# Hybrid recurrent decoder step: first mixer's tiles, second mixer's preparation, first loads and a triangular inverse reordered

## The reference

```python
z = rms(x) @ w_in                      # columns of four mixers and 4 x 1024 merge gates
o_hg = gated linear recurrence (HGRN2) # S = diag(a) S + k v^T, by chunks
o_rw = RWKV-7 delta rule               # S = S diag(w) - (S kk)(kk a)^T + v k^T
o_gl = gated linear recurrence (GLA)
o_ml = stabilised mLSTM                # S with a running maximum, by chunks
mix  = sum_b (o_b @ w_branch[b]) * sigmoid(gate_b) @ w_out
x = x + mix;  x = x + relu(rms(x) @ w_up)**2 @ w_down;  y = rms(x)
```

## Time and profile before

| | |
|---|---|
| median of 3 runs | 2309.73 us (2306.72 to 2310.21) |
| the profiled execution: time, span | 2299.72 us, 2298.2 us |
| mean granted TensorE clock | 0.972 of full speed |
| PE / PEld / DVE / ACT / POOL busy | 94% / 90% / 46% / 26% / 20% |
| chain that ended last | PE 82%, DVE 6%, ACT 4%, DMA 3%, issue 2%, POOL 1% |

### The profile page before, as it was taken

One profiled execution on the slowest core, in us unless ns is written; L12 is line 12 of the kernel. 1 busy time (PEld: TensorE's weight loads), 2 busy tenths in 40 slices (PEclk: granted clock), 3 DMA queues, 4 the chain that ended last, 5 costly groups with the idle time before them and its releaser, 6 DMA issues.

```text
span 2298.2 us, 33450 instructions
## 1 busy us (share of the span) xinstructions
PE 2160.4 (94%) x13459; PEld 2058.7 (90%) x13459; DVE 1054.4 (46%) x1540; ACT 604.8 (26%) x799; POOL 459.4 (20%) x463
## 2 busy tenths in 40 slices
PE   5998998899999897999999999999999999999995
PEld 3997887899999786899999999999999999999994
DVE  4051332467575445443433478642222235656654
ACT  3331221523232143112221243010000013333342
POOL 1122112444454331110000276210000010000012
PEclk9999998999999898999999999999999999999997
DMA  4122123412222240110101475131111224111112
GB/s 157 37 57 61 56 68 70 176 57 61 69 77 62 76 165 29 38 47 20 37 19 37 161 254 187 46 114 44 46 46 46 93 106 165 46 46 37 46 46 84
DMA packets 48563, 177.31 MB, mean 77 GB/s; under 512 B 6401, under 2 KB 6753, under 8 KB 48241
## 3 DMA queue, kind: packets, MB, share of 16 engines
q1 hardware_dynamic: 23040, 85.65, 12.1%
q0 software_dynamic: 17648, 61.31, 7.7%
q10 hardware_dynamic: 7808, 29.41, 3.3%
HBM read 128.84 MB, written 47.51 MB: 77 GB/s over the span
## 4 chain that ended last, share of the span: by engine, by line
PE 82%; DVE 6%; ACT 4%; DMA 3%; issue 2%; POOL 1%; DVEq 0%; SPq 0%; ACTq 0%; POOLq 0%
PE PS L463 25%; PE PS L623 20%; PE PS L1422 15%; PE PS L1384 2%; PE PS L1116 2%; PE PS L1295 2%; PE PS L1291 2%; PE PS L1283 2%; PE PS L1128 1%; DMA RING<-in_w_all 1%; PE PS L983 1%; PE PS L1249 1%; DVE AR L2059 1%; PE PS L1257 1%; POOL RING_parts L458 1%
## 5 line engine op out<-in xcount | busy, mean ns | idle before, releaser
L463 PE MATMUL PS<-HT_parts,WHIA_parts 128*128 128x352 f32 (+1 forms) x1440 | 510.4, 354 | 35.5 <-POOL RING_parts L458 20.0
L463 PE MATMUL PS<-OT_parts,WHIA_parts 128*128 128x352 f32 (+1 forms) x1440 | 477.6, 332 | 0.0
L463 PE MATMUL PS<-HT_parts,RING_parts 128*128 128x352 f32 (+1 forms) x1440 | 476.3, 331 | 0.0
L463 PEld LDWEIGHTS PS<-HT_parts,WHIA_parts 128*128 128x128 f32 x1440 | 280.1, 195 | 50.3 <-POOL RING_parts L458 21.4
L458 POOL TENSOR_TENSOR RING_parts<-RING,WHIA_parts 128x1024 fp32r<-128x1024 f32 x60 | 156.2, 2604 | 809.9 <-ACT WHIA_parts L453 809.9
L463 PEld LDWEIGHTS PS<-OT_parts,WHIA_parts 128*128 128x128 f32 x1440 | 279.4, 194 | 3.7 <-issue 0.2
L463 PEld LDWEIGHTS PS<-HT_parts,RING_parts 128*128 128x128 f32 x1440 | 278.8, 194 | 0.0
L1422 PE MATMUL PS<-MIXHI_parts,CF_parts 128*128 128x352 f32 x768 | 250.5, 326 | 3.4 <-DVEq L2571 2.9
L623 PE MATMUL PS<-HT_parts,CF_parts 128*128 128x352 f32 x768 | 249.7, 325 | 0.9 <-ACT AR L590 0.9
L1422 PE MATMUL PS<-MIXHI_parts,RING_parts 128*128 128x352 f32 x768 | 249.6, 325 | 0.0
L623 PE MATMUL PS<-HT_parts,RING_parts 128*128 128x352 f32 x768 | 248.4, 323 | 0.0
(11 more groups left out here) (394 smaller groups left out, 3607.2 us busy)
## 6 DMA issues: line engine op xcount, KB each, us to landing
RING<-in_w_all SPq DMA_DIRECT2D x132, 512.0 KB, 3.3
AR<-gates POOLq DMA_DIRECT2D x32, 528.0 KB, 4.0
proj<-AR ACTq DMA_DIRECT2D x18, 537.0 KB, 5.0
AR<-proj POOLq DMA_DIRECT2D x18, 537.0 KB, 8.3
gates<-CF ACTq DMA_DIRECT2D x16, 528.0 KB, 5.1
gates<-AR ACTq DMA_DIRECT2D x16, 528.0 KB, 5.1
AR<-in_xT SPq DMA_DIRECT2D x8, 537.0 KB, 14.3
AR<-in_xT POOLq DMA_DIRECT2D x8, 528.0 KB, 5.8
```

The costliest lines, as they stand in the source:

```text
L463: last = e.matmul(out, a_[:, u, k, :], b_[:, k, t], start=first and i == 0, stop=end and i == 2)
```

## The change

Four groups of edits; the arithmetic stays the same but for the order in the inverse. The diff is cut to what is told here.

**Loads first.** The constants before column `bd_gl` (258 of 3909 columns) and the input rows are loaded first; the masks (`in_cu`) and the rest of the constants follow the first weight chunk. The high part of that chunk is made before the norm's root, PE waits for all loads just before the projection, and DVE converts the masks in the middle of its loop.

```diff
                 e.activation(SQB[:, k % 4], XT[:, k, :], ACT.Square, scale=D ** -0.5).then_inc(S("norm_sq"), 1)
+            weight_hi(e, 0, P_ML)
             e.wait_ge(S("sq_used"), KD // 2)
...
-            e.dma_start(CF[:, :], A["cf"]).then_inc(S("consts"), 16)
-            e.dma_start(CUF, A["cu"]).then_inc(S("consts"), 16)
+            first = fcols["bd_gl"][0]
+            e.dma_start(CF[:, 0:first], A["cf"][:, 0:first]).then_inc(S("consts"), 16)
...
-            for u in range(2):
-                load(u, A["w_all"], u)
+            load(0, A["w_all"], 0)
+            e.dma_start(CUF, A["cu"]).then_inc(S("ws"), 16)
+            e.dma_start(CF[:, first:], A["cf"][:, first:]).then_inc(S("ws"), 16)
+            load(1, A["w_all"], 1)
...
-            e.wait_ge(S("ws"), 32)
-            e.wait_ge(S("split0"), P_ML + 1)
+            e.wait_ge(S("ws"), 64)
...
+                if k == 0:
+                    e.wait_ge(S("split0"), P_ML + 1)
```

```diff
-            e.wait_ge(S("out"), 4 * 16)
+            e.wait_ge(S("ml_rows"), 1)
...
+            weight_lo(e, 1, P_FILL + 1)
+            weight_lo(e, 0, P_FILL + 2)
+            e.wait_ge(S("out"), 6 * 16)
             e.memset(SML, 0.0).then_inc(S("zeroed"), 1)
...
                 e.activation(MC[:, :, 0:w], src, ACT.Copy).then_inc(S("ml_copied"), 1)
-                steps(outs, 1)
                 e.wait_ge(S("ml_kt"), n + 1)
...
-                steps(outs, 1)
+                steps(outs, 2)
...
                     last.then_inc(S("ml_ds"), 1)
+                    steps(fill, 4)
+                    back_to_rows(3)
+                    steps(fill, 8)
                     e.wait_ge(S("ml_dsu"), 1)
```

```diff
+            e.wait_ge(S("ml_mt"), 2)
+            for u in range(2):
+                e.wait_ge(S(f"fill_sent{u}"), (Q_GL + 2) * 16)
+            for g in range(2):
+                e.dma_start(GK[:, g], proj_row(2 + g)).then_inc(S("rows0"), 16)
...
-            e.wait_ge(S("out"), 16 * 16)
-            barrier(e, 2)
...
             fill = fill_work(e, Q_RW)
-            steps(fill, 24)
-            join(e, 2)
-            e.wait_ge(S("ws"), 32)
+            steps(fill, 8)
+            e.wait_ge(S("states_final"), 1)
...
-            for u in range(2):
-                e.wait_ge(S(f"fill_sent{u}"), Q_RW * 16)
-            e.wait_ge(S("ml_pre"), TILES + 2)
-            arrive(e)
+            e.wait_ge(S("rows0"), 2 * 16)
+            for g in range(2):
+                log_row(g)
+                steps(outs, 1)
```

```diff
-                    e.wait_ge(S("rw_t"), t0 + (2 if l == 1 else rw_ti(l - 1)))
+                        e.wait_ge(S("rw_t"), t0 + (RW_LOWER if l == 1 else rw_tt(l - 1, False)))
...
+                        side = half(ti[0:w, h * w:h * w + w], lh, False) if last_tile else half(tt[0:w, h * w:h * w + w], lh, True)
...
+                    if not last_tile and RW_FLIPS < l < nlev - 1:
...
+                    steps(gate, 0 if last_tile else 1)
...
+                def flip(at):
+                    e.wait_ge(S("rw_t"), t0 + at)
+                    e.transpose(flat[0], flat[1]).then_inc(S("rw_t"), 1)
...
+                    first_level()
+                    upto = bc(cm[:, w:2 * w].unsqueeze(1), [w, 2, w])
+                    for j in range(2):
+                        ins = e.scalar_tensor_tensor(part(0, j), upto, 0.0, PS(4 + j, 0, 2 * w)[0:w].rearrange("p (i t) -> p i t", i=2),
+                                                     ALU.is_equal, ALU.mult)
...
+                    if flips:
+                        flip(at)
+                        at += 1
```

More of the change, by code:

```diff
@@ L1052, in ml_tile, with back_to_rows @@
                 last.then_inc(S("ml_o"), 1)
+                def back_to_rows(bank):
+                    e.wait_ge(S("ml_on"), n + 1)
+                    for g in range(2):
+                        last = e.transpose(PS(bank, g * P, g * P + w), MON.rearrange("p h c -> p (h c)")[0:w, g * P:g * P + P],
+                                           ident[0:w, 0:w])
+                    last.then_inc(S("ml_ot"), 1)
                 steps(fill, per // 6)
@@ L1068, in ml_tile @@
                 steps(fill, per // 3)
[L1069 to L1073, removed]
+                if not last_tile:
+                    back_to_rows(5)
             with e.Fori(0, TILES // 2) as i:
@@ L1346, in rw_tile @@
                     last.then_inc(S("rw_ds"), 1)
-                steps(gate, 3 if last_tile else 9)
+                steps(gate, 3 if last_tile else 6)
                 if last_tile:
@@ L1441, in _ @@
             rms_act(e, st)
-            weight_hi(e, 0, P_ML)
             for k in range(KD):
@@ new lines, in _ @@
+            e.wait_ge(S("rows0"), 2 * 16)
+            for g in range(2):
+                log_row(g)
+                steps(outs, 1)
+            steps(outs, 1)
+            e.wait_ge(S("states_final"), 1)
+            fill_outs(e, Q_RW, range(0, 1))
+            e.wait_ge(S("gl_z"), 1)
+            e.wait_ge(S("ot_back"), 2 * 16)
+            st.did(e.activation(row3(GB[:, 2]), cols3(0), ACT.Identity, bias=col("gla_gate_b")))
+            fill_outs(e, Q_RW, range(1, 2))
+            st.settle()
@@ new lines, in _ @@
+            log_row(2)
+            fill_outs(e, Q_RW, range(2, 3))
+            e.wait_ge(S("gl_go"), 1)
+            e.activation(GK[:, 0:2], GK[:, 0:2], ACT.Sigmoid, scale=-1.0)
+            fill_outs(e, Q_RW, range(3, 5))
+            e.wait_ge(S("rows2"), 4 * 16)
+            for u in range(2):
+                e.activation(OTG[:, 2 * u:2 * u + 2], OTG[:, 2 * u:2 * u + 2], ACT.Silu)
+                if u == 0:
+                    fill_outs(e, Q_RW, range(5, 6))
+            fill_outs(e, Q_RW + 1, range(0, 1))
@@ L1583, in gl_exps @@
+            exp_ln_table(e)
+            fill_outs(e, Q_RW + 1, range(1, 2))
             def gl_exps(n, last_tile):
@@ L1620, in _ @@
             gl_ends(0, False)
+            fill_outs(e, Q_RW + 1, range(2, 6))
             split = Q_GATE - Q_GL_TILES
@@ L2025, in _, with log_gate, sums @@
             ml_tile(TILES, LASTW, True)
-            barrier(e, 2)
             e.tensor_scalar(OMM, CC[:, COLS["rwkv_mu"][0]:COLS["rwkv_mu"][0] + 8], -1.0, 1.0, ALU.mult, ALU.add)
-            e.wait_ge(S("gl_ln"), 1)
-            st.did(e.scalar_tensor_tensor(GL_, GB, 0.0, GT, ALU.min, ALU.subtract))
-            st.settle()
+            def log_gate(g):
+                e.wait_ge(S("gl_ln"), g + 1)
+                x = GB[:, g] if g == 2 else GK[:, g]
+                st.did(e.scalar_tensor_tensor(GL_[:, g], x, 0.0, GL_[:, g], ALU.min, ALU.subtract))
+                st.settle()
+            def sums(g):
+                st.did(e.tensor_tensor_scan(GB[:, g], keep, GL_[:, g], 0.0, ALU.mult, ALU.add))
+            for g in range(2):
+                log_gate(g)
+            e.sem_inc(S("gl_go"), 1)
+            e.wait_ge(S("ot_back"), 2 * 16)
+            for g in range(2):
+                sums(g)
+            log_gate(2)
             st.did(e.tensor_scalar(GL_[:, 2], GL_[:, 2], 1.0 / 16, None, ALU.mult))
             st.settle()
-            for g in range(3):
-                st.did(e.tensor_tensor_scan(GB[:, g], keep, GL_[:, g], 0.0, ALU.mult, ALU.add))
+            sums(2)
             e.wait_ge(S("rows1"), 4 * 16)
```

184 lines of the change are left out of this document (103 added, 81 removed).

## The result

The changed kernel took 2236.57 us (median of 4 runs, 2233.61 to 2237.69) against 2309.97 for the kernel before (2306.72 to 2315.79): a ratio of 0.9685, interval 0.9665 to 0.9706. The prediction said 2236. Its profiled execution took 2233.61 us. That is 3.0 under its median, while the profiled one of before stood 10.0 under the median that was shown. So of the 73.4 us between the medians only 66.2 can be seen between the two traces, and the 73.3 us of the sum were 7 too many. By the interval of the ratio the change is worth 68 to 77 us.

A forecast was written before the change was run, and what follows sets the result against it. The kernel was taken as bound by PE's list. Terms 9.3 + 11.5 + 8.4 + 21.1 + 7.8 + 15.2 = 73.3 us; 2299.7 - 73.3 = 2226.4, plus 10.0 gives 2236; range 2219 to 2264, the forecast's own 2228 to 2247.

The forecast's parts named there:

- Loads first: Start of the kernel: input rows ahead of most constants let PE's projection begin earlier, 9.3 us, bounds 6 and 11.
- with 10.0 for the median: End of the sum: 10.0 us added because the median shown lay that far above the profiled execution.
- Chunk: Ahead of the mLSTM tiles: POOL's subtraction comes first, so PE's 9.3 us wait and 2.2 more go; 11.5 us.
- Tiles: First mixer: ACT's moved filler bank and chunk copy remove PE's 1.05 us wait at L1042 in eight tiles; 8.4 us.
- Transition: Last mLSTM tile to next mixer: 13.65 us of standing still and 7.5 of slow clock go; 21.1, bounds 10 and 25.
- what is late next: In the transition: POOL's load of eight rows, landing some 4 us before ACT would hold up a bank.
- First tile: First HGRN2/GLA tile: prepared while PE is in filler, it costs what the second does; 7.8 us, bounds 0 and 8.
- Inverse: RWKV tiles: removed products save 3.76 us a tile, new waits cost 1.9; 15.2 us in eight tiles, bounds 0 and 30.
- Gains all: Rival, inverse: moved steps and neighbouring products cover every wait, 30.1 us in place of 15.2, time 2221; chance 0.10.
- gains nothing: Rival, inverse: each level's wait is 0.3 us longer and eats the removed products, time 2251; chance 0.14.
- The late loads: Rival, second mixer: DVE passes hold up POOL's load issues, rows land up to 9 us later; 12 us, 2248; chance 0.11.
- The slow flip: Rival, inverse levels 1 to 5: DVE transposes at 3.5 us eat the whole gain, at 4 us time 2328; chance 0.03.

The follow-up runs named there:

- before_again: The kernel before, unchanged, run and profiled a second time: median 2304.39 us, ratio 0.9994; the second profile took 2303.14 us.
- pool_old: Changed kernel with POOL's old order ahead of the mLSTM tiles (store wait, clearing and state loads before the chunk's subtractions): 2247.14 us, ratio 0.9739.
- act_old: Changed kernel with ACT's filler banks of the first mixer emptied at the places of the kernel before, in all nine tiles: 2245.66 us, ratio 0.9727.
- loads_old: Changed kernel with SP's first loads in the old order, masks and other constants ahead of the input rows: 2238.37 us, ratio 0.9703.
- m_memset: Changed kernel with POOL's clearing of the 128x4608 states moved ahead of the chunk's subtraction in the fifth HGRN2/GLA tile: 2228.07 us, ratio 0.9656.
- inv_old: Changed kernel with the RWKV inverse of the kernel before, including its products, masks and filler step places: 2248.85 us, ratio 0.9745.
- m_last: Changed kernel with ACT emptying its second filler bank ahead of the squares in the last mLSTM tile: 2237.19 us, ratio 0.9679.
- m_all: Changed kernel with m_last, m_memset, POOL's shifted-row store behind a subtraction, and its last HGRN2/GLA expansion behind the masked operands: 2223.07 us, ratio 0.9631.
- inv_steps: Changed kernel with the new inverse, but its filler steps at the places of the kernel before: 2270.68 us, ratio 0.9862.
- barrier: Changed kernel with the barrier between the two mixers put back on PE, ACT, DVE and POOL: 2235.57 us, ratio 0.9679.
- flip4: Changed kernel with every flip of the inverse (DVE's transpose) done four times in a row: 2371.34 us, ratio 1.0243.

## Why the prediction was right, term by term

**The total hides two errors of 7 us that cancel.** The sum was 73.3, the traces show 66.2; the step from profile to median was taken as 10.0 and was 3.0. 2299.7 - 66.1 + 3.0 is the measured 2236.6 (66.1 by the executions' times). That 2236 was met to a microsecond is luck; each error alone would have put it 7 us off. Of the one error the step is "with 10.0 for the median": before_again shows that it was scatter of the executions of one kernel, not a property of it. Of the other the steps are the transition, sized 5.1 us too large, and the 5.3 us that the sum did not have, while tiles, inverse and chunk came out larger than priced. The ratio, made of several runs of both, is the firmer number.

**Loads first**, 9.3: 8.4. DVE began its first scaled row at 26.83 (26.1 forecast), and PE started 1.5 us behind it at 28.32. The constants were not late: the last of them landed at 25.9 (24.5 forecast), and PE's wait there names DVE.

**Chunk**, 11.5: 12.4 in the traces, 12.5 by pool_old. The wait of 9.3 went as priced, and what lay behind it was 3.1 for the 2.2 of the sum.

**Tiles**, 8.4: 10.6. The mechanism is right (act_old), the size was outside the bounds: a tile gained 1.32 us, 1.05 of wait and 0.27 of busy time with the same 94 matmuls (17.08 in 18.14 before; 16.81 of 16.81 now). The granted clock is 1.00 in both, so the 0.27 are not the clock; where they come from is not shown, and as PE's ends are modelled only the 1.32 is firm.

**Transition**, 21.1: 16.0. The clock's part held (mean 0.98 for 0.89 in the earlier trace rows; busy time 6.9 us less, forecast 7.5), the standing still did not go in full: 4.3 us of new waits, and behind the first of them five microseconds (330.57 to 335.57) at a mean clock of 0.66, against the sign that no stretch would be under 0.9. One I had read in the diff and thought harmless, the filler banks behind the squares: in the last tile the products of nine segments lie ahead of those. The other I named as what is late next, with the wrong object. The loads of POOL's eight rows are in time; a weight chunk that is loaded beside them is not. From 340 to 385 us in the changed one (DMA issues, median us to landing; the chunk's median over the whole span is 3.3 us):

```profile
AR<-proj POOLq DMA_DIRECT2D x8, 537.0 KB, 13.1
RING<-in_w_all SPq DMA_DIRECT2D x3, 512.0 KB, 6.1
```

How long this takes differs: from L1092 to the first HGRN2/GLA tile the same code took 55.4 us in the changed one, 55.1 in loads_old, 57.6 in m_memset and 60.3 in inv_old, and 63.0 to 63.3 in the three runs that reach L1092 without the wait for the bank (act_old, m_last, m_all). So one trace gives this term to some 5 us. That these loads delay the chunk is argued from the rows; no run moved them. Nor does a run say which of the edits gave the 16.0.

**First tile**, 7.8: 7.8. It is as long as the second, 38.19 and 38.21.

**Inverse**, 15.2: 17.2, and 13.8 by inv_old's ratio (some 8 either way by the two intervals). Two sizes inside it were off, in the same direction, and nearly cancel. A removed product was priced at 0.94 us; four of them took 2.72 us of PE's busy time (37.66 to 34.94), 0.68 each. The waits were priced at 1.9 us a tile and 0.4 more is seen than before. The level's period, which I had as 3.4 us, is 3.27 (first products 1013.02 and 1016.29), with the flip as forecast at 0.71:

```profile
1013.02 1.00 PE L1310 MATMUL PS<-AR 128*128 128x64 f32 x8
...
1014.57 1.10 PE L1331 MATMUL PS<-AR 128*128 128x64 f32 x8
...
1015.82 0.42 DVE L2468 COPY_PREDICATED AR<-CU,PS 128x256 f32<-128x256 uint8 x1 [2.45 <-PE PS L1331]
...
1016.27 0.71 DVE L2433 STREAM_TRANSPOSE AR<-AR 128x512 f32<-128x512 f32 x1
1016.29 1.10 PE L1310 MATMUL PS<-AR 128*128 128x64 f32 x8
```

PE's ends are modelled, so the split between busy and idle is rough; 2.32 us a tile is not. "The filler steps are only moved" was the weakest sentence: without the move the term is about -27 us, some 18 either way (inv_steps against inv_old).

**Not foreseen**, -5.3, in code that the change leaves alone: 3.5 us of it in the fifth tile (41.52 for 38.04), at POOL's clearing. DVE and POOL arrive there at other times than in the first trace of before, and the clearing falls on the copy. m_memset shows it. But the change is not its cause: before_again shows the same clash in the kernel before (next rows), and in m_last the fifth tile is 38.1 us with no edit there. Against the trace of before_again this term is -2.5, and PE's whole lead 69.5 in place of 66.2 us. The rest lies in the slow clock of the third tile (0.96) and in the preparation of the RWKV mixer, and was not tested.

```profile
643.22 3.19 DVE L2072 COPY AR<-AR 128x384 f32 x1
...
642.16 3.97 POOL L831 MEMSET AR<- 128x4608 f32 x1
```

**The rivals.** Gains all and gains nothing fell with inv_old. The late loads: in the changed one POOL issues the eight rows from 361.59 on, 0.1 us before a pause of DVE's sums, so there was next to nothing to hold them up. In barrier four of them lie beside a sum (rows below) and take no longer than the 2.09 us of the same four in the changed one, so that mechanism is not seen; of its 12 us the transition lacks 5.1, and the waits that show there are others. The slow flip: the price of 3.5 us a flip at which the change would be lost was too high. At 2.9 us flip4 is already slower than the kernel before, and busy time at a low clock, not standing still, is most of that. The range's ends do not come out of the terms named with them: 2228 less 14.9 for the full inverse is 2213, not 2219, and 2251 with 6 and 1 is 2258, not 2264. The result lies inside either pair.

```profile
372.46 4.68 DVE L2089 TENSOR_TENSOR_SCAN AR<-CF,AR 128x1074 f32<-128x1074 f32 x2
...
372.56 2.08 POOL L796 DMA_DIRECT2D AR<-proj  x4
```

## What to carry to other kernels

On an engine that is always busy, look for what stands in another engine's list ahead of the one operand it waits for: a store's wait, a clearing, a bank. That order was worth 12 us at one place here and 6.5 by the ratio at another that the change had left alone, while putting the barrier between the stages back changed the time by nothing that could be measured. When work is taken out of such a list, something must be put where its cover was: the same new inverse was about 14 us faster than the old one with its filler between the levels and about 27 us slower with the filler elsewhere. And take a ratio over many runs, not the distance of one profile from a median, as a term of a sum.

## What was not expected of the hardware

Short stops that recur went here with a loss far larger than themselves. At 2.0 us of stops a tile of 37 (inv_steps) the granted clock went to the lower of its levels, 1.2 GHz, within some tiles and stayed at 2.4 in others with the same instructions (means of 1.00, 0.88, 0.66); with 0.4 us in 35.39 it was 1.00 in seven of the eight full tiles of the changed one, and 0.95 in the first, as in the first of the kernel before. In flip4 it was 0.60 to 0.63 in all eight.

The clock also fell where no stop is seen. In m_last, m_all and barrier it took 336.6 to 336.8 us from the first RWKV tile to the output transposes of the last, in place of 331.1 in the changed one, with no edit there. The loss is all in the last tile, in which PE is never seen idle; that tile in the changed one, then in m_last:

```profile
1178.00:1225.65 47.65, 47.65 (x397) 44.23 (x394) 18.73 (x37) 7.22 (x18) 4.72 (x2) 0.96 0.16 46
```

```profile
1176.66:1229.80 53.14, 53.14 (x396) 49.44 (x392) 18.74 (x37) 7.23 (x18) 4.73 (x2) 0.85 0.13 41
```

What brought the clock down there stays open.

A DVE copy of 128x384 took 3.18 us in place of 0.48 beside a POOL clearing that had begun first, and ended 0.3 us behind it. "SBUF — State Buffer" in the Trainium skill, section "SBUF: two separate sides", has some VectorE instructions, an fp32 copy within SBUF among them, and those of GpSimd share a port pair that whichever starts first holds for its whole instruction. These rows agree.
